# Seven tile widths instead of four for the experts of a hybrid decoder layer

## What is computed

```python
def moe_ffn(h, w_router, b_router, w_gu, b_gu, w_down, b_down):
    t = h.reshape(-1, d)
    logits = (t @ w_router + b_router).astype(jnp.float32)
    top_v, top_i = lax.top_k(logits, TOP_K)
    gates = jax.nn.softmax(top_v, axis=-1)
    ...
    gu = lax.ragged_dot(xs, w_gu, sizes) + b_gu[e_sorted]
    x_glu = jnp.minimum(gu[:, :D_FF], SWIGLU_LIMIT)
    x_lin = jnp.clip(gu[:, D_FF:], -SWIGLU_LIMIT, SWIGLU_LIMIT)
    act = x_glu * jax.nn.sigmoid(SWIGLU_ALPHA * x_glu) * (x_lin + 1.0)
    out = lax.ragged_dot(act, w_down, sizes) + b_down[e_sorted]
    out = out * gates.reshape(-1)[order][:, None].astype(out.dtype)
    y = jnp.zeros_like(t).at[tok].add(out)
```

## Time and profile before

| | |
|---|---|
| median of 3 runs | 5041.88 us (5039.2 to 5041.95) |
| span of the profiled execution | 5040.9 us |
| stages before the experts' first gate/up matmul | 2332.7 us |
| TensorE matmul busy | 4902.0 us, 97% |
| VectorE busy | 2883.7 us, 57% |
| ScalarE busy | 1806.5 us, 36% |
| GpSimd busy | 686.4 us, 14% |
| mean DMA rate | 165 GB/s |

### The profile page before, as it was taken

The page is one execution under the profiler, slowest core; times in us unless marked ns, Lnnn a source line. Parts: engine busy times, 40 slices in busy tenths (PEclk is TensorE's granted clock), DMA queues, the critical chain, the costliest instruction groups (busy, mean ns, idle before and its releaser), DMA issues.

```text
span 5040.9 us, 78669 instructions
## 1 busy us (share of the span) xinstructions
PE 4902.0 (97%) x29176; PEld 4367.5 (87%) x29176; DVE 2883.7 (57%) x5675; ACT 1806.5 (36%) x2807; POOL 686.4 (14%) x647
## 2 busy tenths in 40 slices
PE   8999999999899989997999999999999999999998
PEld 7888888888789978786999999999999999999997
DVE  4343432111566776555556666666677777777776
ACT  4112121111256742232333333343444444444443
POOL 0000000333021002121111011121111111111111
PEclk9999999999999999998999999999999999999999
DMA  4312221322544455444445546455566666666665
GB/s 139 109 65 80 82 84 69 130 89 79 190 164 148 153 164 177 153 144 159 154 142 190 181 150 211 173 187 187 178 224 244 231 231 211 218 234 237 230 219 196
DMA packets 263760, 832.50 MB, mean 165 GB/s; under 512 B 39068, under 2 KB 70039, under 8 KB 226072
## 3 DMA queue, kind: packets, MB, share of 16 engines
q1 hardware_dynamic: 228632, 714.76, 39.3%
q0 software_dynamic: 30064, 98.23, 7.9%
q10 hardware_dynamic: 4896, 17.31, 1.0%
HBM read 671.61 MB, written 163.88 MB: 166 GB/s over the span
## 4 chain that ended last, share of the span: by engine, by line
PE 51%; DVE 1%; issue 1%; ACT 1%; DMA 0%; POOL 0%; POOLq 0%; DVEq 0%; ACTq 0%
PE ex_g L2317 33%; PE ex_d L2331 17%; PE ex_g L2303 1%; DVE ex_xl L2434 1%; ACT ex_xh L2380 0%; DVE ex_y L2475 0%; DVE ex_wgl L2421 0%; DMA ex_xg<-h_d,ex_nxt 0%; DVE ex_t L2448 0%; ACT ex_wgh L2367 0%; POOLq L2194 0%; POOL out L2277 0%; ACT ex_y L2389 0%; DVE ex_bgu L2443 0%; DVE ex_bgu L2442 0%
## 5 line engine op out<-in xcount | busy, mean ns | idle before, releaser
L2317 PE MATMUL ex_g<-ex_xh,ex_wgh 128*128 128x256 f32 (+3 forms) x4352 | 1272.0, 292 | 9.3 <-DVE ex_xl L2434 7.4
L2317 PE MATMUL ex_g<-ex_xh,ex_wgl 128*128 128x256 f32 (+3 forms) x4352 | 1266.9, 291 | 0.0
L2317 PE MATMUL ex_g<-ex_xl,ex_wgh 128*128 128x256 f32 (+3 forms) x4352 | 1266.3, 291 | 0.0
L2317 PEld LDWEIGHTS ex_g<-ex_xh,ex_wgh 128*128 128x128 f32 x4352 | 816.4, 188 | 33.6 <-DVE ex_xl L2434 21.8
L2317 PEld LDWEIGHTS ex_g<-ex_xl,ex_wgh 128*128 128x128 f32 x4352 | 816.6, 188 | 8.7
L2317 PEld LDWEIGHTS ex_g<-ex_xh,ex_wgl 128*128 128x128 f32 x4352 | 817.7, 188 | 0.0
L2367 ACT ACTIVATE ex_wgh<-ex_wg 128x2048 fp32r<-128x2048 f32 x274 | 524.8, 1915 | 375.1 <-PE ex_g L2317 350.5
L2421 DVE TENSOR_TENSOR ex_wgl<-ex_wg,ex_wgh 128x2048 fp32r<-128x2048 f32 x274 | 626.1, 2285 | 18.3 <-ACT ex_wgh L2367 15.5
L2331 PE MATMUL ex_d<-ex_wdh,ex_ath 128*128 128x512 f32 x1312 | 524.0, 399 | 0.0
L2331 PE MATMUL ex_d<-ex_wdl,ex_ath 128*128 128x512 f32 x1312 | 515.6, 393 | 0.0
L2331 PE MATMUL ex_d<-ex_wdh,ex_atl 128*128 128x512 f32 x1312 | 514.5, 392 | 0.0
(11 more groups left out here) (388 smaller groups left out, 7538.8 us busy)
## 6 DMA issues: line engine op xcount, KB each, us to landing
ex_wg<-in_w_gu SPq DMA_DIRECT2D x276, 1024.0 KB, 5.9
ex_wd<-in_w_down SPq DMA_DIRECT2D x276, 512.0 KB, 6.8
qkv_d<-prj_o SPq DMA_DIRECT2D x144, 256.0 KB, 2.0
wo_spare<-qkv_d SPq DMA_DIRECT2D x40, 768.0 KB, 4.3
prj_raw<-in_w_in SPq DMA_DIRECT2D x109, 256.0 KB, 3.3
ex_bd<-in_b_down SPq DMA_DIRECT2D x34, 512.0 KB, 8.7
gate_d<-prj_o SPq DMA_DIRECT2D x64, 256.0 KB, 2.0
mix_ring<-gate_d SPq DMA_DIRECT2D x32, 512.0 KB, 4.1
```

The costliest lines, as they stand in the source:

```text
L2317: last = pe.matmul(gu[j][:, 0:size], w[:, k, j, :], x[:, k, 0:size], start=(k == 0 and x is xh and w is h), stop=(k == KD - 1 and w is l))
```

## The change

- The widths become 384, 336, 304, 288, 272, 256 and 232. One comparison of all counts with all limits gives the class of each.
- A rest of over 384 rows becomes a tile of 256 and a tile of what is left, in the width that fits it. The table gets one more column with a limit on the rows that count. In the expert stage GpSimd fetches it by a small DMA per tile and multiplies the gates with a mask (position under the limit), since a loop that must run once could take such a tile with three groups.
- In tiles of two groups GpSimd gathers two groups of the next tile's rows instead of three.
- The table has 66 rows instead of 128, and there are seven loop bodies instead of four.

```diff
-LARGE, MIDDLE, NARROW, SMALL = 384, 320, 288, 256
-SIZES = (LARGE, MIDDLE, NARROW, SMALL)
+SIZES = (384, 336, 304, 288, 272, 256, 232)
+LARGE, HALF = SIZES[0], 256
+NK = len(SIZES)
...
-TW = 2 + len(SIZES)
+TW = 3 + NK
+TILES = 2 * NE + 2
...
+                for k in range(NK):
+                    pool.memset(limit[:, k:k + 1], float(SIZES[k + 1]) if k + 1 < NK else 0.0).then_inc(iot, 1)
...
+                chain(tsc(two[:, :], rest[:, :], float(LARGE), None, ALU.is_gt))
+                chain(stt(over[:, :], rest[:, :], -float(HALF), two[:, :], ALU.add, ALU.mult))
+                chain(tt(rest[:, :], rest[:, :], over[:, :], ALU.subtract))
+                tt(above[:, :, :], by_class(rest), limits, ALU.is_gt)
+                chain(tt(before[:, :, :], by_class(over), limits, ALU.is_gt))
+                chain(tt(above[:, :, :], above[:, :, :], before[:, :, :], ALU.add))
+                tt(both[:, 0, :], above[:, 0, :], full[:, :], ALU.add)
+                chain(tt(both[:, 1:, :], above[:, 1:, :], above[:, 0:NK - 1, :], ALU.subtract))
+
+                chain(dve.tensor_tensor_scan(flat(upto), junk[:, 0:NK * NE], flat(both), 0.0, ALU.mult, ALU.add))
...
+                def limit(i):
+
+                    pool.dma_start(lim[:, :], table_d[ds(i, 1), TW - 1:TW].to_broadcast([P, 1])).then_inc(lim_in, 16)
+
+                def fetch(i, ng, first=False):
...
+                        limit(i)
                         stop_until(pool, sl_in, 16 * i, tick)
                         stop_until(pool, turned, B6 * i, tick)
-                    for g in range(G3):
+                    for g in range(ng):
...
                 def tile(i, ng):
                     stop_until(pool, g_in, 16 * G3 * i + 16 * G3, tick)
+                    stop_until(pool, lim_in, 16 * i + 16, tick)
                     pool.tensor_copy(cur[:, :, 0], nxt[:, :, 0])
-                    pool.tensor_copy(cur[:, :, 1].bitcast(F32), nxt[:, :, 1].bitcast(F32)).then_inc(cur_ready, 1)
+                    pool.tensor_scalar(inside[:, :], pos[:, :], lim[:, :].bitcast(F32), None, ALU.is_lt).then_inc(inside_ready, 1)
+                    stop_until(pool, inside_ready, i + 1, tick)
+                    pool.tensor_tensor(cur[:, :, 1].bitcast(F32), nxt[:, :, 1].bitcast(F32), inside[:, :],
+                                       ALU.mult).then_inc(cur_ready, 1)
                     stop_until(pool, cur_ready, i + 1, tick)
-                    fetch(i + 1)
+                    fetch(i + 1, ng)
```

More of the change, by code:

```diff
@@ L1820, in route @@
         cnt, two = (t_.sb(n, [P, NE]) for n in ("cnt", "two"))
-        both, upto, before = (t_.sb(n, [P, len(SIZES) * NE]) for n in ("both", "upto", "before"))
-        row, ei, nth, second, tail, later, third, last_ = (t_.sb(n, [P, 1]) for n in (
-            "row", "ei", "nth", "second", "tail", "later", "third", "last"))
+        full, rest, over = (t_.sb(n, [P, NE]) for n in ("full", "rest", "over"))
+        limit = t_.sb("limit", [P, NK])
+        both, upto, before, above = (t_.sb(n, [P, NK, NE]) for n in ("both", "upto", "before", "above"))
+        row, ei, nth, kind, own, later, whole, at, pair = (t_.sb(n, [P, 1]) for n in (
+            "row", "ei", "nth", "kind", "own", "later", "whole", "at", "pair"))
+        end = t_.sb("end", [P, NK])
         tab = t_.sb("tab", [P, TW])
@@ L2102, in _ @@
                 dve.wait_ge(cnt_mm, 1)
-                full, middle, narrow, small = (both[:, n * NE:(n + 1) * NE] for n in range(len(SIZES)))
-                dve.memset(junk[:, 0:len(SIZES) * NE], 1.0)
+                flat = lambda t: t[:, :, :].rearrange("p k e -> p (k e)")
+                by_class = lambda t: t[:, :].unsqueeze(1).to_broadcast([P, NK, NE])
+                limits = limit[:, :].unsqueeze(2).to_broadcast([P, NK, NE])
+                dve.memset(junk[:, 0:NK * NE], 1.0)
                 chain(dve.tensor_copy(cnt[:, :], pr[:, 0:NE]))
-                chain(tsc(full, cnt[:, :], 2.0 * SMALL, None, ALU.is_gt))
+                chain(tsc(full[:, :], cnt[:, :], 2.0 * HALF, None, ALU.is_gt))
@@ L2109, in _ @@
                 for j in range(1, REGION // LARGE):
[L2110 to L2143, removed]
@@ new lines, in _ @@
+                tt(end[:, :], upto[:, :, NE - 1], ecol[:, 0:NK], ALU.subtract)
+                chain(tsc(flat(before), flat(upto), row[:, :], None, ALU.is_le))
+                chain(dve.tensor_reduce(ei[:, :], flat(before), AX.X, ALU.add))
+                chain(tt(flat(before), flat(before), flat(upto), ALU.mult))
+                chain(dve.tensor_reduce(nth[:, :], flat(before), AX.X, ALU.max))
+                tt(nth[:, :], row[:, :], nth[:, :], ALU.subtract)
+                chain(tsc(above[:, 0, 0:NK - 1], ecol[:, 1:NK], float(NE), ei[:, :], ALU.mult, ALU.is_le))
@@ new lines, in _ @@
+                chain(dve.tensor_reduce(kind[:, :], above[:, 0, 0:NK - 1], AX.X, ALU.add))
+                tsc(later[:, :], kind[:, :], 1.0, None, ALU.is_ge)
+                tsc(whole[:, :], kind[:, :], float(SIZES.index(HALF)), None, ALU.is_equal)
+                chain(stt(own[:, :], kind[:, :], -float(NE), ei[:, :], ALU.mult, ALU.add))
+                tsc(full[:, :], full[:, :], later[:, :], float(LARGE), ALU.mult, ALU.mult)
+                chain(tsc(rest[:, :], ecol[:, :], own[:, :], None, ALU.is_equal))
@@ new lines, in _ @@
+                chain(tt(over[:, :], two[:, :], rest[:, :], ALU.mult))
+                chain(dve.tensor_reduce(pair[:, :], over[:, :], AX.X, ALU.add))
+                chain(tt(pair[:, :], pair[:, :], whole[:, :], ALU.mult))
+                chain(stt(at[:, :], nth[:, :], 1.0, pair[:, :], ALU.subtract, ALU.mult))
+                tsc(tab_i[:, TW - 1:TW].bitcast(F32), at[:, :], float(LARGE - HALF), float(LARGE), ALU.mult, ALU.add)
+                chain(tt(whole[:, :], later[:, :], whole[:, :], ALU.subtract))
@@ new lines, in _ @@
+                tsc(two[:, :], two[:, :], whole[:, :], float(HALF), ALU.mult, ALU.mult)
+                chain(tsc(later[:, :], later[:, :], float(HALF - LARGE), float(LARGE), ALU.mult, ALU.add))
+                chain(tt(full[:, :], full[:, :], two[:, :], ALU.add))
+                tt(nth[:, :], nth[:, :], later[:, :], ALU.mult)
+                chain(tt(full[:, :], full[:, :], rest[:, :], ALU.mult))
+                chain(dve.tensor_reduce(at[:, :], full[:, :], AX.X, ALU.add))
+                chain(tt(nth[:, :], nth[:, :], at[:, :], ALU.add))
@@ new lines, in _ @@
+                chain(stt(tab[:, 1:2], own[:, :], float(REGION), nth[:, :], ALU.mult, ALU.add))
+                chain(tsc(tab[:, 1:2], tab[:, 1:2], float(NE * REGION), None, ALU.min))
+                tsc(tab[:, 0:1], own[:, :], float(NE - 1), None, ALU.min)
+                chain(dve.tensor_tensor_scan(tab[:, 2:2 + NK], junk[:, 0:NK], end[:, :], 1.0, ALU.mult, ALU.max))
+                chain(tt(tab[:, 2:2 + NK], tab[:, 2:2 + NK], ecol[:, 0:NK], ALU.add))
+                dve.tensor_copy(tab_i[:, 0:2 + NK], tab[:, 0:2 + NK]).then_inc(fin, 1)
@@ L2282, in tile @@
                     pool.sem_inc(y_free, 1)
-                fetch(0, True)
+                pool.wait_ge(pos_ready, 1)
+                fetch(0, G3, True)
+                limit(0)
                 ends = numbers(pool)
```

30 lines of the change are left out of this document (15 added, 15 removed).

## The result

The changed kernel takes 5007.64 us (median of 4 runs, 5005.58 to 5010.06), the kernel before 5041.91 (5039.2 to 5043.51). The ratio is 0.9931, with a 95% interval of 0.9919 to 0.9943. It is faster by 34 us. The forecast was 4982 with a range of 4973 to 5024, so the way and the range hold, but 26 us of the 60 that were forecast are missing. The time lies outside 4973 to 4992, to which the forecast gave 0.74. It is in the part of the range that was there for the first rival. In the profiled executions the span falls from 5040.9 to 5004.0 us.

The account below looks back on a forecast made before the run. TensorE, busy 97% of the span, was taken as the bound, so width is time. -20.2 - 41.2 + 1.7 = -59.7 us on 5040.9 gave 4981.2, forecast as 4982 us; range 4973 to 5024, with 0.74 on 4973 to 4992.

Parts of the forecast that it names:

- the first rival: Gate/up matmuls: the weight load already sets 117.8 ns, so 232 columns gain nothing; 5023 us, chance 0.14 with partial gains.
- What bounds the kernel, and the tiles: TensorE carries 97% of the span, so width is time; routing gives 34 tiles, thirteen of them of 232.
- Three-group tiles, -20.2 us: Expert-stage tiles over 256 wide: new widths 336, 304 and 272 change tile times, in sum -20.2 us.
- The line through 288 and 256: Gate/up matmul time against width: 0.44 ns a column, 7.0 ns for the 16 columns from 288 to 272.
- Thirteen tiles of 232, -41.2 us: Narrowest expert tiles: 3.17 us saved in each of thirteen against 256 columns, with ends 0 and -49.
- I take 109 ns, the row nearest in kind: Price of a 232-column gate/up matmul, taken from transposes with one weight load each; 117.8 ns at 256.
- The first step behaved as forecast: First step of a 232 tile: VectorE's clip ends it, TensorE follows at 5.58 us, gaining 0.2, not 0.4.
- the one with a slow mode: Matmuls at 232 columns leave the one-pass fp32r rate: about 6520 us, or 5470 in one instruction; chance 0.09.
- The table, +1.5 us: VectorE's table work at the end of routing grows with arrays of 224 elements: +1.5 us, between 0.5 and 3.
- the +0.2 for three more semaphores: End of the kernel: three more semaphores to clear cost +0.2 us.
- GpSimd, nothing: Expert stage: GpSimd's extra DMA, compare and multiply cost nothing, hidden in its 39.7 us wait for ScalarE's scaled rows.
- the three signs that the prediction named as wrong: A piece of 48 staying at 5.66 us or rising, TensorE waiting for gathers, or its clock below full in the expert stage.

Follow-up runs that it names:

- the old places: The changed kernel with every expert-stage array back at its SBUF address from the kernel before: 4998.15 us, ratio 0.9911 to the kernel before.

## Why the prediction was nearly right, and where it was not

**What bounds the kernel, and the tiles.** Right. Widths and counts came out as counted, TensorE still carries 97%, and nothing new stands on the path.

**Three-group tiles, -20.2 us.** Right in sum at the old places, where the tile of 336 takes 94.97 us (95.15 forecast), 304 takes 89.42 (89.9) and 272 takes 85.54 (85.0): the errors cancel to 0.2 us. The first step of a 272 tile is ended by VectorE as forecast: it lasts 6.76 us at 272 and 6.77 at 288, and the groups by shape of the changed kernel have 1.6 us of waits for the clip at 272. The line through 288 and 256, which gave 124.9 ns at 272, was too low at the old places (6.09/48 = 126.9).

**Thirteen tiles of 232, -41.2 us.** This term was mis-sized. It is -27.4 at the old places (13 x 2.11, the gap between the two runs with and without 232). The step that failed is "I take 109 ns, the row nearest in kind": the mechanism, one weight load per matmul, was the right one, and the trace's transposes gave its size as 109, but between fp32r products of high and low parts it costs 111.6. A tile gained 2.11 us, 1.06 less than forecast. In seven steps the 2.6 ns make 0.9 us of that (336 matmuls). Two small terms make the rest: the second step takes 5.43 us and not 5.36, and the down products of these tiles take 2.78 us each step against 2.757 in the tiles of 256, 0.15 us a tile. The cause of these two stays open. The first step behaved as forecast: 5.52 us (5.58 forecast). It is ended by VectorE's clip: the next matmul starts 0.15 us after the end of the clip, as it does in the tiles of 272 and 288. At 232 that makes 0.17 us from one start to the next in place of 0.11; the groups by shape put down no wait for it. The rival that 117.8 ns is already the floor, and the one with a slow mode, are out: 240 columns go at 111.6 ns and 128 columns at 110.6.

**The table, +1.5 us.** Right. VectorE at the end of routing, as in the earlier trace rows:

```profile
2296.60 0.13 DVE L2114 COPY rt_cnt<-rt_r 128x32 f32<-128x32 f32 x1
...
2299.72 0.39 DVE L2128 TENSOR_TENSOR rt_above<-rt_above,rt_before 128x224 f32<-128x224 f32 x1
...
2300.65 0.62 DVE L2132 TENSOR_TENSOR_SCAN rt_upto<-rt_junk,rt_both 128x224 f32<-128x224 f32 x1
...
2307.50 0.17 DVE L2171 CAST rt_tab_i<-rt_tab 128x9 int32<-128x9 f32 x1
```

From the first to the last it is 11.07 us where it was 9.71: +1.4 for the +1.5 of the table. A step on 224 elements takes 0.39 us, the scan 0.62. No run shows the +0.2 for three more semaphores by itself; from the start of the last tile to the end it is 89.0 us where it was 89.3.

**GpSimd, nothing.** Right. In order of time, the work of a 232 tile, answering to the earlier trace rows:

```profile
4664.16 0.19 POOL L2304 TENSOR_TENSOR ex_cur<-ex_nxt,ex_inside 128x3 f32<-128x3 f32 x1 [0.18 <-POOL ex_inside L2302]
4665.82 0.87 POOL L2287 DMA_DIRECT2D ex_nxt<-slots_d  x1 [1.47 <-issue]
4667.28 0.60 POOL L2279 DMA_DIRECT2D ex_lim<-table_d  x1 [0.59 <-issue]
...
4716.21 2.34 POOL L2310 DMA_INDIRECT out<-ex_y,ex_cur  x1 [41.86 <-ACT ex_y L2425]
```

It waits 41.9 us before its scatter, longer than the 39.7 of before; one gather of three is gone. Of the three signs that the prediction named as wrong none came: TensorE waits for no gather between tiles, the granted clock is full in the expert stage, and a piece of 48 is not at 5.66 us but at 5.35.

**What no step had.** The prediction took each shape of before at its old time. That step, too, failed: the smaller table buffer and the small new arrays moved the big arrays against each other, a cost that the sum put at nothing. It is 0.45 us in each of seven 256 tiles, 0.86 in three of 288, 1.0 in two of 304, 0.5 in five of 336, 0.14 in thirteen of 232, and -0.5 in three of 272. Summed over the two traces that is 10.8 us of tile time, and 9.5 us between the medians with the new and the old places.

**The account of the spans.** The forecast was 4981.2, the trace has 5004.0. That is 22.8 more. The tiles of 232 at the old places give +14.2 (1.09 us each), the places +10.8, the other tiles -0.1 and the table -0.1, in all 24.8. The 2.0 us too many are of the size of what differs from run to run: the first tile took 103.2 us here and 104.6 before, and the table's work began 2.0 us earlier. That the time came out inside the range is in part luck: the range reached up to 5023 for a floor at 117.8 ns, which is not there, and that room took in the places, which no term had.

## What to carry to other kernels

Narrowing a matmul pays only down to the width at which the load of its weights takes over; measure that width with one kernel whose steps differ only in it, before choosing tile sizes, and put the smallest size right there. When an edit changes the size or the order of on-chip buffers, compare the time of the shapes that did not change: if it moved, keep the old distances of the big operands and put new small arrays behind them. A test that moves one array by a gap should also take back what the gap does to the arrays behind it. Where a first step of a tile is ended by another engine, count its gain only up to that engine's end.

## What the runs showed of the hardware that was not expected

- fp32r matmuls with a 128x128 weight load each stand 117.8 ns apart at 256 columns, 111.6 at 240 and 110.6 at 128; with 64 stationary columns it goes down to 58 ns. So the last 16 columns before 256 cost 6 ns, nearly what the slope of the wider ones gives (0.43 ns a column, from 173.3 at 384 to 117.8 at 256), and the next 112 cost 1 ns together.
- Moving arrays by 32 bytes against each other changes the pitch of unchanged matmuls by up to 2.6% (6.63 to 6.80 us for 48 of 304 columns), in both directions: in the changed kernel 272 columns gain 2% where 256 lose 0.7%. Moving all of them together changes nothing.
- In the kernel before, with the same instructions on the engines, the new places cost 17 us, 0.33%.
